# Moving the raw and the split weight rings of an encoder trunk to lower SBUF addresses, behind the activation buffers

## The chip, the core and the metric

The kernel runs on one core of one Trainium2 chip. The metric is the device time of one execution in microseconds; the text compares medians of several runs. One execution was also recorded by the hardware profiler, and everything said about single instructions comes from that recording.

## The reference

Two layers of a bidirectional hybrid encoder on a sequence of 256 positions with 2048 channels, all in float32, followed by a final RMSNorm. What matters for the time are the matrix products:

```python
hn = rms_norm(x, norm_w)
u = jnp.einsum("bsd,dn->bsn", hn, w_in) + b_in          # 2048 x 20496
q, k, v, o, z_a, gates, glu_a, glu_b, z_b, g_a, g_b = jnp.split(u, _OFFSETS, axis=-1)
...
y_a = jnp.einsum("bsw,wd->bsd", ya, w_a)                # 2048 x 2048, after a two-way mLSTM
y_b = jnp.einsum("bsw,wd->bsd", c, w_b)                 # 2048 x 2048, after a 31-tap convolution
merged = jax.nn.sigmoid(g_a) * y_a + jax.nn.sigmoid(g_b) * y_b
return x + jnp.einsum("bsd,de->bse", merged, w_out)     # 2048 x 2048
```

Between them stand four mLSTM heads of 512 channels in both directions, two depthwise convolutions, norms and gates.

## The kernel before, in words

**Split operands.** Every weight and every activation of the large products is split into a high part (rounded to the matmul's reduced 4-byte type, float32r) and a low part (what is left). A product is high x high + high x low + low x high. The activations lie in `Hs` (the normed input, later the merged branches) and `YC` (the branch outputs): 16 channel tiles of 512 columns each, 256 high ones and then 256 low ones.

**Pairs.** The unit of work is a pair of 128-column blocks of a weight matrix, 104 pairs in a layer and 208 in all. A pair's weights, 2048 rows by 256 columns, come in four quarters (`c` = 0 to 3) of 4 channel tiles each. SP loads a quarter into the raw ring `RAW` (L299, 512 KB). ACT casts it to the high part `WH` (L389), DVE subtracts that from the raw one for the low part `WL` (L690); both are halves of the split ring `W`. Each ring holds four quarters, one of each `c`, so quarter `c` of the next pair may be loaded and split as soon as TensorE has finished quarter `c` of this one. Semaphores carry this: `raw_in`, `hi_made`, `lo_made`, `multiplied`.

**The order long, long, short, short.** In `multiply` the weights are the stationary operand and the activations stream. For each channel tile TensorE runs two matmuls of 512 columns (high weights against both activation parts, one for each of the two blocks), then two of 256 columns (low weights against the high activations). Such a set of four is called a group below; a pair has 16 groups, and 192 of the 208 pairs run this way, 3072 groups.

```python
1250                    for kk in range(KQ):
...
1254                        for t in range(2):
1255                            mm(ps[:, 2 * q + t, :], WH[:, c, kk, t * P:t * P + P], act_in[:, kt, :],
1256                               start=(kt == 0), stop=False)
1257                        for t in range(2):
1258                            i = mm(ps[:, 2 * q + t, S:2 * S], WL[:, c, kk, t * P:t * P + P],
1259                                   act_in[:, kt, 0:S], start=False, stop=(kt == KT - 1))
```

**The turned order.** The other 16 pairs (two for each head, the values of the mLSTM) go through `multiply_turned`. There the activations are stationary and the weights stream, and a long matmul (L1274) alternates with a short one (L1276), 32 such twos in a pair, 512 in all. The 512 columns of the long one are two blocks of 256, one of `WH` and one of `WL`.

**The gate product.** Once in a layer the 16 gate columns of `w_in` are multiplied (L1334 and L1335): 16 times a long and a short matmul in turn, the stationary operand in `YC`, the streaming one in `Hs`. Neither touches the rings.

**Around them** stand small full-float32 matmuls in `px` (scores, L1393 and L1414; spreads and sums, L1320, L1384). ACT evicts and activates, DVE adds, convolves and norms.

**Addresses.** `sb` allocates the buffers one behind the other, in the order of the code (L122 to L146), and every buffer lies in all 128 partitions at the same byte offset. The order of the instructions on each engine doesn't depend on it.

Of the kernel before, what the change touches and what calls it, by code (L numbers as in the profile page):

```python
# [31 lines left out]
F32R = mybir.dt.float32r  # L32
# [4 lines left out]
P = 128  # L37
# [18 lines left out]
QC = 4  # L56
KQ = KT // QC
PC = 2 * P
# [53 lines left out]
def build_trunk(nc, x, norm_w, w_in, b_in, qk_conv_w, mlstm_norm_w, w_a, dw_w, dw_b,  # L112
                ln_w, ln_b, w_b, w_out, final_norm_w, out):
    with ExitStack() as ctx:
        def sb(name, shape, dt=F32):
            return ctx.enter_context(nc.sbuf_tensor(name, shape, dt))
# [5 lines left out]
        X = sb("X", [P, KT, S])  # L122
        Hs = sb("Hs", [P, KT, 2 * S], F32R)
        YC = sb("YC", [P, KT, 2 * S], F32R)
        CP = sb("CP", [P, KT * CW + PAD])
        M = sb("M", [P, KT, S])
        HEAD = sb("HEAD", [P, KT, S])
# [5 lines left out]
        ACC = sb("ACC", [P, 2, S])  # L133
        CWT = sb("CWT", [P, 2, DW_TAPS + 1])
        RR = sb("RR", [P, S])
        RAW = sb("RAW", [P, QC, KQ, PC])
        W = sb("W", [P, QC, 2, KQ, PC], F32R)
        PAR = sb("PAR", [P, L * PARS + KT])
        IDENT = sb("IDENT", [P, P])
        ONES = sb("ONES", [P, P])  # L140
# [6 lines left out]

        WH, WL = W[:, :, 0, :, :], W[:, :, 1, :, :]
        K_, V_, SO_ = (HEAD[:, HT * i:HT * (i + 1), :] for i in (0, 2, 3))
# [4 lines left out]

        GS = YC[:, 0:KT // 2, :].rearrange("p k (a g) -> p (k a) g", a=2)
        GLOW, GATES = HEAD[0:NG, 2 * HT + 1, :], HEAD[0:NG, 2 * HT + 2, :]
# [3 lines left out]
        SQUARES = HEAD[:, :, :].rearrange("p (s a) b -> p s (a b)", s=ST)  # L160
        PROWS = CP[:, 0:(L * PBLK + 1) * P].rearrange("p (b c) -> p b c", c=P)

# [95 lines left out]
        def conv_in(tile, tap):  # L258

            return CP[:, ds(tile * CW + tap, S)]  # L260

        def conv_out(tile, count):

            return CP[:, tile * CW:(tile + count) * CW].rearrange(
                "p (t c) -> p t c", c=CW)[:, :, PAD:CW]
# [5 lines left out]
        def buf(g):  # L271

            return (EW, QB)[g % 2]
# [9 lines left out]
        def _(sp):  # L283
# [10 lines left out]
            def load_pair(w, l, col, n):  # L294

                for c in range(QC):

                    sp.wait_ge(lo_made, n * QC + (c + 1))
                    sp.dma_start(RAW[:, c, :, :], w[l, :, c * KQ:(c + 1) * KQ, ds(col, PC)]  # L299
                                 ).then_inc(raw_in[c], 16)  # L300
# [40 lines left out]
        def _(pool):  # L341
# [5 lines left out]
                                    ).then_inc(ident_made, 1)  # L347
            nc.gpsimd.memset(YC[:, 0:KT // 2, :].bitcast(F32), 0.0).then_inc(gs_clear, 1)
            steps.mark(nc.gpsimd.memset(GC[:], 0.0))
            steps.mark(nc.gpsimd.memset(QPAD[:], 0.0))  # L350
            pool.wait_ge(rows_turned, 1)
            steps.mark(nc.gpsimd.memset(CP[:, 0:KT * CW].rearrange("p (t c) -> p t c", c=CW)
                                        [:, :, 0:PAD], 0.0))
            steps.mark(nc.gpsimd.memset(CP[:, KT * CW:], 0.0))
            steps.wait()
            pool.sem_inc(pads_made, 1)
            with pool.Fori(0, L) as l:

                n0 = pool.snap(l * NP)
                for c in range(QC):  # L360
                    pool.wait_ge(hi_made, n0 * QC + (c + 1))
                    nc.gpsimd.tensor_tensor(out=WL[:, c, :, :], in0=RAW[:, c, :, :],
                                            in1=WH[:, c, :, :].bitcast(F32), op=ALU.subtract
# [20 lines left out]
        def _(act):  # L384
            def split_hi(n, c):

                act.wait_ge(raw_in[c], n * 16 + 16)
                act.wait_ge(multiplied, n * QC + (c + 1))
                nc.scalar.copy(WH[:, c, :, :], RAW[:, c, :, :]).then_inc(hi_made, 1)  # L389

# [57 lines left out]
            with act.Fori(0, L) as l:  # L448
# [50 lines left out]
                with act.Fori(0, H) as h:  # L499
# [46 lines left out]
                    act.wait_ge(ya_made, u + 1)  # L546
                    nc.scalar.copy(YC[:, ds(h * HT, HT), 0:S], KV_).then_inc(ya_hi, 1)  # L547

# [36 lines left out]
                def cb_high(g):  # L585
                    act.wait_ge(cb_made, l * 4 + (g + 1))
                    nc.scalar.copy(YC[:, 4 * g:4 * g + 4, 0:S], buf(g)[:]).then_inc(cb_hi, 1)

# [94 lines left out]
        def _(dve):  # L683
# [3 lines left out]
            def split_lo(n, c):  # L687

                dve.wait_ge(hi_made, n * QC + (c + 1))
                v.tensor_tensor(WL[:, c, :, :], RAW[:, c, :, :], WH[:, c, :, :].bitcast(F32),  # L690
                                ALU.subtract).then_inc(lo_made, 1)
# [45 lines left out]
            with dve.Fori(0, L) as l:  # L737
# [59 lines left out]
                def glu_mul(tile, unit):  # L797

                    dve.wait_ge(glu_sig, unit)
                    dst = CP[:, ds(tile * CW, 2 * CW)].rearrange("p (t c) -> p t c", c=CW)  # L800
                    steps.mark(v.tensor_tensor(dst[:, :, PAD:CW], QB[:, 0:2, :], QB[:, 2:4, :],
# [79 lines left out]
                with dve.Fori(0, H) as h:  # L881
# [145 lines left out]
                    for t in range(HT):  # L1027
                        if t % 2 == 0:
# [6 lines left out]
                    dve.wait_ge(ya_hi, u + 1)  # L1035
                    v.tensor_tensor(YC[:, ds(h * HT, HT), S:2 * S], KV_,
                                    YC[:, ds(h * HT, HT), 0:S].bitcast(F32), ALU.subtract
                                    ).then_inc(ya_lo, 1)
# [198 lines left out]
        def _(pe):  # L1237
# [24 lines left out]
            def multiply_turned(n, k):  # L1262
# [3 lines left out]
                for c in range(QC):  # L1266
# [3 lines left out]
                    for kk in range(KQ):  # L1270
                        kt = c * KQ + kk
                        for s in range(ST):
                            bank = ps[:, 2 * q + s, :].rearrange("p (a b) -> p a b", a=2)
                            mm(bank, Hs[:, kt, s * P:(s + 1) * P], W[:, c, :, kk, :],  # L1274
                               start=(kt == 0), stop=False)
                            i = mm(bank[:, 1, :], Hs[:, kt, S + s * P:S + (s + 1) * P],  # L1276
                                   W[:, c, 0, kk, :], start=False, stop=(kt == KT - 1))
                    i.then_inc(multiplied, 1)
# [214 lines left out]
```

## Time and profile before

| what | before |
|---|---|
| median of 3 runs | 2509.46 us (2509.41 to 2509.69) |
| profiled execution, its own time | 2509.14 us |
| its span, first to last instruction | 2507.4 us |
| mean granted TensorE clock | 0.994 |
| busy: PE / PE weight loads / DVE / ACT | 99% / 86% / 77% / 52% |
| weights read from HBM | 441.59 MB in 2.5 ms |

The span is that of the instructions; the execution's time is 1.7 us longer. PE is TensorE streaming, PEld its weight loads, which lie beside the streaming. A matmul's recorded length contains its way through the array, which the next one overlaps, so the pace is read from starts, not from lengths.

### The profile page before, as it was taken

To read this page: it belongs to the slowest core of one execution; us is meant where nothing else is said; L and a number is where in the kernel's file an instruction comes from. 1 tells how busy PE (TensorE), PEld (TensorE's weight loads), DVE (VectorE), ACT (ScalarE), POOL (GpSimd) and SP (SyncE) were. 2 spreads that over 40 slices of the span, in tenths; PEclk is the share of its full clock that TensorE was granted. 3 is DMA by queue.
4 is the path that set the end of the run, shared out by engine and by line. 5 is a ranking of instruction groups with operands and counts; after the bars stand their busy time and mean duration, and the time that the engine had idled before them with its cause. 6 is when DMAs were issued, how large, how long until landed. Compare 5 with 4: busy or idle time off the path is not lost.

```text
span 2507.4 us, 43931 instructions
## 1 busy us (share of the span) xinstructions
PE 2474.0 (99%) x14063; PEld 2158.4 (86%) x14063; DVE 1937.5 (77%) x2872; ACT 1316.2 (52%) x1574; POOL 55.6 (2%) x43
## 2 busy tenths in 40 slices
PE   7999999999999999999989999999999999999998
PEld 6888888888888888888878888888888888888887
DVE  5788989898978786556568888888888877765565
ACT  4545454545465557555354454545454655665543
POOL 2000000000000000000010000000000000000000
PEclk9999999999999999999999999999999999999999
DMA  6566656565656666665546656555565666666654
GB/s 185 170 187 184 177 164 182 163 182 165 180 175 186 188 180 186 190 185 190 172 124 188 190 177 178 170 174 176 168 183 159 186 186 186 176 195 187 185 183 134
DMA packets 447922, 444.95 MB, mean 177 GB/s; under 512 B 17968, under 2 KB 445760, under 8 KB 447808
## 3 DMA queue, kind: packets, MB, share of 16 engines
q1 hardware_dynamic: 447808, 443.74, 59.3%
q8 instruction: 34, 0.56, 0.1%
q14 instruction: 80, 0.66, 0.1%
HBM read 441.59 MB, written 2.10 MB: 177 GB/s over the span
## 4 chain that ended last, share of the span: by engine, by line
PE 95%; issue 2%; DVE 2%; ACT 1%; SPq 0%; DVEq 0%; DMA 0%; ACTq 0%
PE ps L1255 55%; PE ps L1258 28%; PE ps L1274 5%; PE ps L1276 2%; PE px L1414 1%; PE px L1393 1%; PE px L1320 1%; DVE Hs L751 0%; DVE HEAD L1030 0%; PE px L1384 0%; SPq L289 0%; PE px L1334 0%; ACT YC L547 0%; ACT W L389 0%; PE px L1401 0%
## 5 line engine op out<-in xcount | busy, mean ns | idle before, releaser
L1255 PE MATMUL ps<-Hs,W 128*128 128x512 f32 x5120 | 1620.2, 398 | 9.0 <-DVE Hs L751 9.0
L690 DVE TENSOR_TENSOR W<-RAW,W 128x1024 fp32r<-128x1024 f32 x824 | 1019.3, 1243 | 439.8 <-ACT W L389 434.9
L389 ACT CAST W<-RAW 128x1024 fp32r<-128x1024 f32 x832 | 865.7, 1047 | 926.1 <-PE ps L1258 819.4
L1258 PEld LDWEIGHTS ps<-Hs,W 128*128 128x128 f32 x5120 | 964.1, 188 | 231.2
L1258 PE MATMUL ps<-Hs,W 128*128 128x256 f32 x5120 | 1024.6, 281 | 0.0
L1255 PEld LDWEIGHTS ps<-Hs,W 128*128 128x128 f32 x5120 | 790.7, 189 | 14.7 <-DVE Hs L751 10.8
L792 DVE SCALAR_TENSOR_TENSOR ACC<-CP,CWT,ACC 128x256 f32<-128x256 f32 x928 | 388.4, 478 | 0.0
L1255 PE MATMUL ps<-YC,W 128*128 128x512 f32 x1024 | 321.7, 395 | 0.0
L1258 PEld LDWEIGHTS ps<-YC,W 128*128 128x128 f32 x1024 | 192.3, 188 | 46.1
L1258 PE MATMUL ps<-YC,W 128*128 128x256 f32 x1024 | 204.6, 281 | 0.0
L1274 PE MATMUL ps<-W,Hs 128*128 128x512 f32 x512 | 179.9, 393 | 0.0
L1255 PEld LDWEIGHTS ps<-YC,W 128*128 128x128 f32 x1024 | 157.6, 188 | 0.0
L1276 PE MATMUL ps<-W,Hs 128*128 128x256 f32 x512 | 144.3, 282 | 0.0
L402 ACT ACTIVATE T<-ps,PAR 128x256 f32<-128x256 f32 x288 | 119.6, 465 | 0.0
L1274 PEld LDWEIGHTS ps<-W,Hs 128*128 128x128 f32 x512 | 96.1, 188 | 19.9
L1276 PEld LDWEIGHTS ps<-W,Hs 128*128 128x128 f32 x512 | 96.7, 189 | 0.2
L697 DVE TENSOR_TENSOR QB<-ps,T 128x512 f32<-128x512 f32 x112 | 76.5, 683 | 0.8 <-ACT T L398 0.8
L906 DVE SCALAR_TENSOR_TENSOR HEAD<-QPAD,PAR,HEAD 128x256 f32<-128x256 f32 x128 | 58.3, 524 | 0.2
L446 ACT ACT_TABLE_LOAD x42 | 53.9, 1283 | 0.8
L906 DVE SCALAR_TENSOR_TENSOR QB<-QPAD,PAR,QB 128x256 f32<-128x256 f32 x128 | 52.8, 480 | 1.4 <-DVE QB L906 1.4
L389 ACT ACT_TABLE_LOAD x38 | 48.8, 1283 | 0.7
L446 ACT ACTIVATE QB<-QB 128x512 f32<-128x512 f32 x48 | 30.3, 632 | 18.7 <-DVE QB L697 18.3
(179 smaller groups left out, 978.4 us busy)
## 6 DMA issues: line engine op xcount, KB each, us to landing
RAW<-in_w_in_dram SPq DMA_DIRECT2D x640, 512.0 KB, 3.7
RAW<-in_w_a_dram SPq DMA_DIRECT2D x64, 512.0 KB, 3.4
RAW<-in_w_b_dram SPq DMA_DIRECT2D x64, 512.0 KB, 3.4
RAW<-in_w_out_dram SPq DMA_DIRECT2D x64, 512.0 KB, 4.0
M<-in_x_dram SPq DMA_DIRECT2D x2, 1024.0 KB, 8.4
HEAD<-in_b_in_dram SPq DMA_DIRECT2D x8, 256.0 KB, 3.6
out_dram<-M SPq DMA_DIRECT2D x4, 512.0 KB, 2.9
CP<-in_dw_w_dram SPq DMA_DIRECT2D x3, 128.0 KB, 4.2
```

What stands on the lines that cost most here:

```text
L389: nc.scalar.copy(WH[:, c, :, :], RAW[:, c, :, :]).then_inc(hi_made, 1)
L402: i = nc.scalar.activation(T[:, q, t, :], ps[:, 2 * q + t, S:2 * S], ACT.Identity, bias=bias(t))
L446: nc.scalar.activation(where, where, ACT.Sigmoid).then_inc(done, 1)
L690: v.tensor_tensor(WL[:, c, :, :], RAW[:, c, :, :], WH[:, c, :, :].bitcast(F32), ALU.subtract).then_inc(lo_made, 1)
L697: v.tensor_tensor(dst, ps[:, 2 * q:2 * q + 2, 0:S], T[:, q, :, :], ALU.add).then_inc(pairs_out, 1)
L792: steps.mark(v.scalar_tensor_tensor(out=dst, in0=src, scalar=w, in1=ACC[:, t, :], op0=ALU.mult, op1=ALU.add))
L906: ins = v.scalar_tensor_tensor(out=dst[:, t, :], in0=src, scalar=w, in1=dst[:, t, :], op0=ALU.mult, op1=ALU.add)
L1255: mm(ps[:, 2 * q + t, :], WH[:, c, kk, t * P:t * P + P], act_in[:, kt, :], start=(kt == 0), stop=False)
L1258: i = mm(ps[:, 2 * q + t, S:2 * S], WL[:, c, kk, t * P:t * P + P], act_in[:, kt, 0:S], start=False, stop=(kt == KT - 1))
L1274: mm(bank, Hs[:, kt, s * P:(s + 1) * P], W[:, c, :, kk, :], start=(kt == 0), stop=False)
L1276: i = mm(bank[:, 1, :], Hs[:, kt, S + s * P:S + (s + 1) * P], W[:, c, 0, kk, :], start=False, stop=(kt == KT - 1))
L1320: i = mm(px[:, bank, at + s * P:at + (s + 1) * P], columns[:, s:s + 1].to_broadcast([P, P]), IDENT[:], start=True, stop=True)
```

## The change

Two lines move up. Nothing else differs: every engine has the same instructions in the same order.

```diff
         Hs = sb("Hs", [P, KT, 2 * S], F32R)
         YC = sb("YC", [P, KT, 2 * S], F32R)
+        RAW = sb("RAW", [P, QC, KQ, PC])
+        W = sb("W", [P, QC, 2, KQ, PC], F32R)
         CP = sb("CP", [P, KT * CW + PAD])
...
         RR = sb("RR", [P, S])
-        RAW = sb("RAW", [P, QC, KQ, PC])
-        W = sb("W", [P, QC, 2, KQ, PC], F32R)
         PAR = sb("PAR", [P, L * PARS + KT])
```

The byte offsets within a partition, as the two programs are built:

| buffer | bytes | before, starts at | changed, starts at | start modulo 1024, before / changed |
|---|---|---|---|---|
| X | 16,384 | 16,512 | 16,512 | 128 / 128 |
| Hs | 32,768 | 32,896 | 32,896 | 128 / 128 |
| YC | 32,768 | 65,664 | 65,664 | 128 / 128 |
| RAW | 16,384 | 168,352 | 98,432 | 416 / 128 |
| W | 32,768 | 184,736 | 114,816 | 416 / 128 |
| CP to RR (ten buffers) | 69,920 | 98,432 | 147,584 | all moved by 49,152, unchanged modulo 1024 |
| PAR and the rest | 8,708 | 217,504 | 217,504 | unchanged |

## Rows read from the trace of the kernel before

**Rows 1.** The page: span, busy time of each engine, busy tenths in 40 slices

```profile
span 2507.4 us, 43931 instructions
PE 2474.0 (99%) x14063; PEld 2158.4 (86%) x14063; DVE 1937.5 (77%) x2872; ACT 1316.2 (52%) x1574; POOL 55.6 (2%) x43
PE   7999999999999999999989999999999999999998
```

**Rows 2.** The page: the chain that ended last, by engine, by line

```profile
PE 95%; issue 2%; DVE 2%; ACT 1%; SPq 0%; DVEq 0%; DMA 0%; ACTq 0%
PE ps L1255 55%; PE ps L1258 28%; PE ps L1274 5%; PE ps L1276 2%; PE px L1414 1%; PE px L1393 1%; PE px L1320 1%; DVE Hs L751 0%; DVE HEAD L1030 0%; PE px L1384 0%; SPq L289 0%; PE px L1334 0%; ACT YC L547 0%; ACT W L389 0%; PE px L1401 0%
```

**Rows 3.** Busy time by window: an uninterrupted stretch in either layer

```profile
core 0: us, PE busy (x) PEld busy (x) DVE busy (x) ACT busy (x) POOL busy (x), PEclk, DMA share, GB/s
928.08:1252.70 324.62, 324.62 (x1850) 283.07 (x1849) 194.86 (x190) 180.58 (x214) 0.00 (x0) 1.00 0.61 186
2167.93:2492.54 324.61, 324.61 (x1850) 283.05 (x1849) 194.85 (x190) 180.57 (x214) 0.00 (x0) 1.00 0.58 179
```

**Rows 4.** Timeline of PE (start, length, line): first and last groups of the latter

```profile
2167.92 0.63 PE L1255 MATMUL ps<-Hs,W 128*128 128x512 f32 x2
...
2492.55 0.63 PE L1255 MATMUL ps<-Hs,W 128*128 128x512 f32 x2
```

**Rows 5.** What PE waited for, whole span, longest first (us, times, longest)

```profile
PE ps L1255 <- DVE Hs L751: 9.0, 6, 3.4
PE ps L1289 <- DMA M<-in_x_dram: 8.1, 1, 8.1
```

**Rows 6.** Timeline of PE: one turned pair, first, second and last long matmul

```profile
265.35 0.39 PE L1274 MATMUL ps<-W,Hs 128*128 128x512 f32 x1
265.58 0.28 PE L1276 MATMUL ps<-W,Hs 128*128 128x256 f32 x1
...
276.10 0.39 PE L1274 MATMUL ps<-W,Hs 128*128 128x512 f32 x1
```

**Rows 7.** Timeline of PE: the gate product, second to last long matmul

```profile
38.80 0.40 PE L1334 MATMUL px<-Hs,YC 128*128 128x512 f32 x1
39.03 0.28 PE L1335 MATMUL px<-Hs,YC 128*128 128x256 f32 x1
...
43.75 0.40 PE L1334 MATMUL px<-Hs,YC 128*128 128x512 f32 x1
```

**Rows 8.** Groups of PE by line in 2167.93 to 2492.54

```profile
L1255 PE MATMUL ps<-Hs,W 128*128 128x512 f32 x668 | 209.8, 395 | 0.0
L1258 PE MATMUL ps<-Hs,W 128*128 128x256 f32 x670 | 133.9, 281 | 0.0
L1255 PE MATMUL ps<-YC,W 128*128 128x512 f32 x256 | 80.4, 395 | 0.0
```

**Rows 9.** Timeline of PEld: one load to each matmul

```profile
270.78 0.19 PEld L1274 LDWEIGHTS ps<-W,Hs 128*128 128x128 f32 x1
270.90 0.19 PEld L1276 LDWEIGHTS ps<-W,Hs 128*128 128x128 f32 x1
271.13 0.19 PEld L1274 LDWEIGHTS ps<-W,Hs 128*128 128x128 f32 x1
```

**Rows 10.** The splits of ACT and DVE, whole span, and who waits

```profile
L690 DVE TENSOR_TENSOR W<-RAW,W 128x1024 fp32r<-128x1024 f32 x824 | 1019.3, 1243 | 439.8 <-ACT W L389 434.9
L389 ACT CAST W<-RAW 128x1024 fp32r<-128x1024 f32 x832 | 865.7, 1047 | 926.1 <-PE ps L1258 819.4 <-PE ps L1276 97.5 <-DMA RAW<-in_w_in_dram 5.2
L1036 DVE TENSOR_TENSOR YC<-HEAD,YC 128x1024 f32 x8 | 9.8, 1225 | 1.9 <-ACT YC L547 1.9
ACT W L389 <- DMA RAW<-in_w_in_dram: 5.2, 6, 1.0
```

## The prediction

> **What bounds the kernel now.** First the page: PE is busy 99% of the span and in every slice but the first and a few others full [rows 1]. The chain that ended last is PE for 95%, and 83% of it are the two lines of the long, long, short, short order, 7% the two turned ones [rows 2]. So I asked next whether PE waits there or is simply streaming. In two stretches of 324.6 us, one in each layer, PE has no idle time at all, at a granted clock of 1.00 (the 2.4 GHz level) [rows 3]. The longest waits of PE in the whole span are 9.0 and 8.1 us in total [rows 5]. Nothing feeds PE too late. What is left is the pace of the stream itself, and that has to be read from starts, since lengths overlap.
>
> The second stretch runs from 2167.92 to 2492.55 us [rows 4]. By the code it holds 15 groups of one pair, 64 of the four z_B pairs and 384 of the 24 pairs of g_B, w_B and w_out, 463 starts and so 462 intervals: 324.63 / 462 = 702.7 ns for a group of 2 x 512 + 2 x 256 = 1536 columns. At one column for each beat of 2.4 GHz it would be 640 ns. The stream thus loses 62.7 ns in a group, 9%, or 15.7 ns for each matmul. It is this loss, 3072 x 62.7 ns = 193 us of the kernel, that placement could touch.
>
> **The change part by part.** It removes no instruction and adds none; it moves none on any engine, SP's and POOL's queues included. It changes addresses only. Who touches the moved bytes:
>
> *DMA into RAW, ACT's cast, DVE's subtraction.* The cast takes 1047 ns on average and the subtraction 1243 ns; a subtraction of the same size between buffers that start at 128 modulo 1024 takes 1225 ns [rows 10]. If the rings' new start had any effect here, 18 ns x 824 = 15 us of DVE would go. It counts as nothing, because the work is covered: within the two stretches DVE is busy 195 and ACT 181 of 325 us [rows 3], and the cast waited 917 us for PE to release the ring, against 5.2 us for the load [rows 10]. What would uncover it: in a group time of 0.70 us a quarter takes PE 2.8 us, the load share is 0.61 [rows 3], and the cast and the subtraction one after the other take 2.3 us but run three quarters ahead. They would have to be slowed by far more than the 18 ns in question. The bound above and below is 0 us.
>
> *The ten buffers CP to RR* move by 49,152 bytes and keep their start modulo 1024. They are read and written by the small work, of which only the float32 matmuls in px lie on the chain, about 1% a line [rows 2]. I take 0; they run a fixed sequence, and no row shows one of them depending on an address.
>
> *PE's own reads of W.* This is the only term with a price. Is there a row which shows that the pace depends on where operands lie? Three streams can be compared, all of 4-byte float32r, all with one weight load beside each matmul [rows 9]:
> - the group order, W stationary (start 416 modulo 1024), Hs streaming (128): 702.7 ns, so 351.3 ns for a long and a short [rows 4];
> - the turned order, Hs stationary (128), W streaming (416): 31 intervals from 265.35 to 276.10, 346.8 ns [rows 6];
> - the gate product, YC stationary (128), Hs streaming (128): 14 intervals from 38.80 to 43.75, 353.6 ns [rows 7].
>
> The last two have the same order (long, short), the same column counts and the same clock, and differ by 6.8 ns, 2%. They differ in the operands: roles, the split of the long stream into two blocks, and placement. So the pace is not fixed by shape alone. What does not matter is also visible. In the gate product the distance between the two operands changes with every step by 1024 bytes, and in a pair it runs through four values of kk and, between Hs and YC, through a further 32,768 bytes; yet the mean length with YC is 395 ns as with Hs [rows 8]. Large steps of distance are therefore without effect. What the change does alter is the small part: W goes from 416 to 128 modulo 1024, the phase that YC and Hs have. It makes every pair of operands lie like those of the gate product, which is the slowest of the three.
>
> I bound the term by these rows. Upper row: the group order takes the pace of the gate product, 2 x 353.6 = 707.2 ns, +4.5 ns x 3072 = +13.8 us, and the turned one too, +6.8 ns x 512 = +3.5 us; sum +17.3 us. Lower row: the group order takes the turned pace, 693.6 ns, -9.1 x 3072 = -28.0 us, the turned one stays. Above the upper row: if the phase costs the group order the same factor that separates the two alternating streams, 353.6 / 346.8 = 1.020, it is 716.5 ns, +42.4 us, with the turned term +46 us. Below the lower one: all of the loss goes, -193 us, and 512 x (346.8 - 320) = -14 us.
>
> I take the upper row, +17.3 us, because it is the one stream in the trace that lies as all of them will. The sum is made against the profiled execution: 2509.1 + 17.3 = 2526.4 us; that execution stands 0.3 us under the median of the runs, which changes nothing. Everything lies on the path, since PE never waits where the groups run.
>
> A rule speaks against this. The Trainium skill, in the page TensorE: Matmul & The Clock Gate, section Part 2: What happens when you issue a matmul, says that the weight load and the streaming operand have independent read ports, so that loading the next weights takes no read bandwidth from the running matmul. By it placement is worth nothing and the sum is 0. The same page's section Back-to-back issue gap gives N / 2.4 + 2.5 ns, 650 ns for a group, and the trace does not agree with that for this type: 702.7 ns. No run here shows yet what makes the difference.
>
> **The rivals.**
>
> *The pace doesn't depend on the placement* (the change has no effect): 2509 us. For it: the pace is steady over all kk, both activation buffers and both layers [rows 3, 8], and the 6.8 ns can come from the two-block stream or from the roles alone. Against it: there is a loss of 9% that the column count doesn't explain, and an operand-dependent difference of 2%. The rule on read ports above is this rival's.
>
> *The phase was the costly thing before, and falls away*: the reads of W started 32 bytes off a 64-byte boundary, now they start on one as all other buffers do. If such a start costs a part of each weight load or stream, the group order goes down to the turned pace: 2481 us. For it: the group order alone has W stationary, and it loses more than the turned one. Against it: the gate product has no odd start and is slower still [rows 7]. It decides if a group falls under 702 ns.
>
> *The whole loss is a collision* between the two reads of PE that new addresses avoid: 2509 - 207 = 2302 us. Against it: the gate product has other distances and loses as much.
>
> *The phase costs the group order the full factor*: 2555 us. This is the forecast's mechanism at its upper price.
>
> *A feeder becomes the bound*, because DMA, ACT and DVE now work in the bytes next to those that PE streams: it would show as waits of PE for `lo_made`. Against it: the slack above, and the two stretches have the same pace whatever DVE and ACT do. Under 1%, and it is in no case below.
>
> **How the numbers follow.** A change of 0.2%, 5 us, is about what a measurement of this kernel can tell from none. The forecast, 2526 us, has 0.37; the same mechanism at the full factor 0.08. No dependence has 0.27, the odd start falling away 0.24, the whole loss going 0.04. So slower by over 0.2% is 0.45, within 0.2% 0.27, faster 0.28. The range reaches from a little under the turned pace, 2478 us, to the full factor, 2556 us; left out are the case of 2302 us and what lies beyond either end, together under 0.2. As cases of both signs hold much of the chance: the forecast's own range is 2515 to 2540 us.
>
> **What would show it right or wrong.** In the changed profile the instruction counts and the granted clock should be the same, and PE should still have no idle time in the long stretches. Right: a group of 705 to 710 ns, and a turned two of 353 ns instead of 347; the gate product unchanged at 353.6 ns, since neither of its operands moved. If the group moves but the turned two doesn't, it is the stationary read that feels the address; if only the turned one moves, the streaming read. A group at 702.7 ns means no dependence, one near 693 ns the odd start. The forecast fails as a whole if the time changes while the pace of the groups doesn't: then a wait has come up that I excluded. The casts and subtractions may come out some ns shorter or longer, without any effect on the end.

## The result, and the profile after

The changed kernel is faster: a median of 2492.49 us (2491.69 to 2493.51, four runs) against 2509.43 us (2507.43 to 2509.69, four runs) of the kernel before beside it, a ratio of 0.9932 with a 95% interval of 0.992 to 0.9945. That is 17 us less; the forecast was 17 us more.

The page first: the span, busy times and busy slices of PE of the changed kernel.

```profile
span 2490.0 us, 43931 instructions
PE 2455.4 (99%) x14063; PEld 2141.2 (86%) x14063; DVE 1934.5 (78%) x2872; ACT 1317.2 (53%) x1574; POOL 55.6 (2%) x43
PE   7999999999999999999989999999999999999998
```

The same instructions, the same shares as in [rows 1], 17.4 us less span, and 18.6 us less busy time of PE. Now the two long stretches by window (busy time and count of each engine, clock, DMA share, GB/s), which answer to [rows 3]:

```profile
921.36:1243.21 321.85, 321.85 (x1850) 280.81 (x1849) 194.55 (x190) 180.86 (x214) 0.00 (x0) 1.00 0.61 187
2153.45:2475.30 321.85, 321.85 (x1850) 280.81 (x1849) 194.57 (x190) 180.84 (x214) 0.00 (x0) 1.00 0.59 180
```

PE is busy without a break again, at the same granted clock of 1.00, with the same counts; DVE and ACT do the same work in the same time. Only the stretch is 2.8 us shorter. The timeline of PE gives the pace, first and last group of the second stretch, as in [rows 4]:

```profile
2153.44 0.40 PE L1255 MATMUL ps<-Hs,W 128*128 128x512 f32 x1
...
2475.30 0.40 PE L1255 MATMUL ps<-Hs,W 128*128 128x512 f32 x1
```

321.86 / 462 = 696.7 ns for a group, where it was 702.7 ns. 3072 groups x 6.0 ns = 18.4 us: that is the whole result, and a little more.

A little more, because the turned pairs went the other way, in part. Two of them, first and last long matmul from the second one on (30 intervals between the rows):

```profile
262.02 0.39 PE L1274 MATMUL ps<-W,Hs 128*128 128x512 f32 x1
...
272.42 0.39 PE L1274 MATMUL ps<-W,Hs 128*128 128x512 f32 x1
```

```profile
385.01 0.40 PE L1274 MATMUL ps<-W,Hs 128*128 128x512 f32 x1
...
395.61 0.40 PE L1274 MATMUL ps<-W,Hs 128*128 128x512 f32 x1
```

10.40 / 30 = 346.7 ns and 10.60 / 30 = 353.3 ns. In the kernel before all 16 turned pairs ran at 346.7 to 347.1 ns. Here eight run at one of these paces and eight at the other, 512 x 3.0 ns = 1.5 us lost. 18.4 - 1.5 = 16.9 us is what was measured, to within half a microsecond.

And the gate product, whose operands the change doesn't touch, changed its pace (14 intervals):

```profile
38.56 0.39 PE L1334 MATMUL px<-Hs,YC 128*128 128x512 f32 x1
...
43.42 0.39 PE L1334 MATMUL px<-Hs,YC 128*128 128x512 f32 x1
```

4.86 / 14 = 347.1 ns against 353.6 ns in [rows 7]. (With two decimals over 14 intervals the quotient is good to 0.7 ns; the starts to the nanosecond give 346.6 ns.) This row should have stayed. It was the first sign that the row on which the forecast was built isn't what I took it for.

The splits stood still: subtraction 1243 ns and cast 1048 ns, against 1243 and 1047 in [rows 10].

```profile
L690 DVE TENSOR_TENSOR W<-RAW,W 128x1024 fp32r<-128x1024 f32 x824 | 1018.1, 1243 | 426.0 <-ACT W L389 420.4
L389 ACT CAST W<-RAW 128x1024 fp32r<-128x1024 f32 x832 | 866.5, 1048 | 905.3 <-PE ps L1258 795.1 <-PE ps L1276 99.1 <-DMA RAW<-in_w_in_dram 5.3
```

### The profile page after: what moved, and what is told of

The parts are those of the page before. It is cut to its first block, busy times and chain, and to the rows that moved or that the text cites. A ratio compares the mean times of both kernels' runs of the same rounds, so it can differ in the third digit from the quotient of the medians.

```text
span 2490.0 us, 43931 instructions
## 1 busy us (share of the span) xinstructions
PE 2455.4 (99%) x14063; PEld 2141.2 (86%) x14063; DVE 1934.5 (78%) x2872; ACT 1317.2 (53%) x1574; POOL 55.6 (2%) x43
## 4 chain that ended last, share of the span: by engine, by line
PE 95%; issue 2%; DVE 2%; ACT 1%; SPq 0%; DVEq 0%; DMA 0%; ACTq 0%
PE ps L1255 55%; PE ps L1258 27%; PE ps L1274 5%; PE ps L1276 2%; PE px L1414 1%; PE px L1393 1%; PE px L1320 1%; DVE Hs L751 0%; DVE HEAD L1030 0%; PE px L1384 0%; SPq L289 0%; PE px L1334 0%; ACT YC L547 0%; ACT W L389 0%; PE px L1401 0%
## 5 line engine op out<-in xcount | busy, mean ns | idle before, releaser
L1255 PE MATMUL ps<-Hs,W 128*128 128x512 f32 x5120 | 1617.7, 397 | 9.6 <-DVE Hs L751 9.6
L690 DVE TENSOR_TENSOR W<-RAW,W 128x1024 fp32r<-128x1024 f32 x824 | 1018.1, 1243 | 426.0 <-ACT W L389 420.4
L389 ACT CAST W<-RAW 128x1024 fp32r<-128x1024 f32 x832 | 866.5, 1048 | 905.3 <-PE ps L1258 795.1
L1258 PE MATMUL ps<-Hs,W 128*128 128x256 f32 x5120 | 1007.2, 278 | 0.0
L1255 PEld LDWEIGHTS ps<-Hs,W 128*128 128x128 f32 x5120 | 781.6, 189 | 15.2 <-DVE Hs L751 11.2
L1255 PE MATMUL ps<-YC,W 128*128 128x512 f32 x1024 | 321.6, 395 | 0.0
L1255 PEld LDWEIGHTS ps<-YC,W 128*128 128x128 f32 x1024 | 155.9, 189 | 0.0
```

## The experiments

"Distance" below is the start of W less the start of Hs, modulo 256; YC and Hs stand in the same phase. The kernel before has 32, the changed one 0.

### Chance, region, or the small part of the start

The two kernels once more, unchanged:

> The kernel before once more, unchanged, as its own profile beside the others. If the pace of the stream is a property of the program (theories 1 and 2), it shows again 702.7 ns for a group, 346.8 ns for a turned two and 353.6 ns for a two of the gate product, and 2509 us. If the pace is a state that an execution or a chip falls into by chance (theory 3), some of these numbers differ and the time can come near 2492 us.

> The changed kernel once more, unchanged. Theories 1 and 2: a group of 696.7 ns, a two of the gate product of 346.7 ns, 2492 us, ratio 0.993. Theory 3 (a state by chance): the paces can be those of the kernel before, 2509 us.

Then the change taken apart. The rings low, but in the old phase:

```diff
         YC = sb("YC", [P, KT, 2 * S], F32R)
+        sb("GAP0", [P, 72])
         RAW = sb("RAW", [P, QC, KQ, PC])
         W = sb("W", [P, QC, 2, KQ, PC], F32R)
+        sb("GAP1", [P, 184])
         CP = sb("CP", [P, KT * CW + PAD])
```

> The rings stay behind the activation buffers, but 288 bytes further on, so that RAW and W start at 416 modulo 1024 as in the kernel before; all other buffers keep their start modulo 1024. Theory 1 (the small part of the start counts, 416 against 128): the pace of the kernel before, a group of 702.7 ns and a two of the gate product of 353.6 ns, 2509 us, ratio 1.000. Theory 2 (the region counts, behind the activations against the top): the pace of the changed kernel, 696.7 ns, 2492 us, ratio 0.993. Theory 3 (chance): no rule.

The rings high, but in the new phase:

```diff
         RR = sb("RR", [P, S])
+        sb("GAP0", [P, 184])
         RAW = sb("RAW", [P, QC, KQ, PC])
         W = sb("W", [P, QC, 2, KQ, PC], F32R)
+        sb("GAP1", [P, 72])
         PAR = sb("PAR", [P, L * PARS + KT])
```

> The rings stay at the top as in the kernel before, but 736 bytes further on, so that RAW and W start at 128 modulo 1024 as in the changed kernel. Theory 1 (the small part of the start): the pace of the changed kernel, a group of 696.7 ns, 2492 us, ratio 0.993. Theory 2 (the region): 702.7 ns, 2509 us, ratio 1.000. Theory 3 (chance): no rule.

Measured beside the kernel before (2510.15 us): before again 2509.30 us, after again 2493.81 us, low in the old phase 2510.39 us (ratio 1.0001, 0.9989 to 1.0012), high in the new phase 2493.79 us (0.9936, 0.9914 to 0.9959). The timelines of PE over the same 462 groups, first of the rings low in the old phase, then high in the new one (in both the added lines make L1257 of L1255):

```profile
2168.59 0.40 PE L1257 MATMUL ps<-Hs,W 128*128 128x512 f32 x1
...
2493.22 0.39 PE L1257 MATMUL ps<-Hs,W 128*128 128x512 f32 x1
```

```profile
2154.32 0.40 PE L1257 MATMUL ps<-Hs,W 128*128 128x512 f32 x1
...
2476.17 0.40 PE L1257 MATMUL ps<-Hs,W 128*128 128x512 f32 x1
```

324.63 / 462 = 702.7 ns and 321.85 / 462 = 696.6 ns, the 696.7 ns of the changed kernel to within the rounding of the rows. The move of some 70,000 bytes is worth nothing; the part of the start below 1024 is worth all of it. The group pace isn't chance either: two profiles of each kernel gave the same 702.7 and 696.7 ns. But the gate product was. In the second profile of the changed kernel it reads

```profile
38.89 0.40 PE L1334 MATMUL px<-Hs,YC 128*128 128x512 f32 x1
...
43.84 0.40 PE L1334 MATMUL px<-Hs,YC 128*128 128x512 f32 x1
```

4.95 / 14 = 353.6 ns, the pace of the kernel before, with the addresses of the run that showed 347.1.

### Which bytes, and whose

Four kernels from the changed one. A gap of 32 bytes ahead of the rings, then one of 448 (in these and in all later ones a second gap, behind W or, with RAW alone, ahead of it, makes up 1024 bytes with the first and so keeps the other buffers' phase):

```diff
-        RAW = sb("RAW", [P, QC, KQ, PC])
-        W = sb("W", [P, QC, 2, KQ, PC], F32R)
+        sb("GAP0", [P, 8]); RAW = sb("RAW", [P, QC, KQ, PC])
+        W = sb("W", [P, QC, 2, KQ, PC], F32R); sb("GAP2", [P, 248])
```

> The changed kernel with a gap of 32 bytes ahead of RAW: RAW and W start at 160 modulo 1024, on an odd multiple of 32 bytes, the activations at 128. Theory 1a (what counts is the 32-byte bit, whether the start is a multiple of 64): slow as before, a group of 702.7 ns, 2510 us. Theory 1b (a larger part of the distance counts, such as the 256 in the 288 between 416 and 128): a group of 696.7 ns or another number, 2493 us.

> The changed kernel with a gap of 448 bytes (64 + 128 + 256) ahead of RAW: the starts stay multiples of 64 but RAW and W stand at 576 modulo 1024, the activations at 128. Theory 1a (only the 32-byte bit counts): fast, a group of 696.7 ns, 2493 us. Theory 1b (the larger bits count): not 696.7 ns; 702.7 ns and 2510 us if any difference from the activations' phase is what costs.

The gap of 32 bytes ahead of Hs instead, so that all operands shift together:

```diff
-        Hs = sb("Hs", [P, KT, 2 * S], F32R)
+        sb("GAP3", [P, 8]); Hs = sb("Hs", [P, KT, 2 * S], F32R)
```

> The changed kernel with a gap of 32 bytes ahead of Hs: Hs, YC, RAW and W all start at 160 modulo 1024, on an odd multiple of 32 bytes, and have the same phase to each other. Theory A (the relation of the two operands that TensorE reads counts): fast, a group of 696.7 ns, 2493 us. Theory B (each operand's own start counts, a start off a multiple of 64 costs): slow, a group of 702.7 ns or more, 2510 us or above since now the streaming operands are odd too, and the gate product, which had never an odd operand, gets a pace it has not shown yet.

And RAW alone in the old phase:

```diff
-        RAW = sb("RAW", [P, QC, KQ, PC])
-        W = sb("W", [P, QC, 2, KQ, PC], F32R)
+        sb("GAP0", [P, 72]); RAW = sb("RAW", [P, QC, KQ, PC])
+        sb("GAP1", [P, 184]); W = sb("W", [P, QC, 2, KQ, PC], F32R)
```

> The changed kernel with RAW alone at 416 modulo 1024 and W at 128. TensorE never reads RAW. If the effect is in TensorE's reads of W (my theory), it is fast, a group of 696.7 ns, 2493 us. If it comes from the DMA's writes of RAW or from the cast and the subtraction that read it, it is slow, 702.7 ns and 2510 us.

Beside the kernel before at 2509.79 us: 32 bytes 2509.12 us, 448 bytes 2478.92 us (ratio 0.9874, 0.9845 to 0.9903), all shifted 2492.97 us (0.9938), RAW alone 2491.64 us (0.9934). The timelines, of the one with 448 bytes and of the one with all shifted:

```profile
2141.24 0.40 PE L1255 MATMUL ps<-Hs,W 128*128 128x512 f32 x1
...
2460.04 0.39 PE L1255 MATMUL ps<-Hs,W 128*128 128x512 f32 x1
```

```profile
2154.87 0.40 PE L1255 MATMUL ps<-Hs,W 128*128 128x512 f32 x1
...
2476.73 0.40 PE L1255 MATMUL ps<-Hs,W 128*128 128x512 f32 x1
```

318.80 / 462 = 690.0 ns, and 321.86 / 462 = 696.7 ns. Two readings follow. The kernel with every operand on an odd multiple of 32 bytes is as fast as the one with none: what counts is the distance between TensorE's two operands, not the start of either (theory A; tried at one distance, 0, and with one shift, 32 bytes). And RAW, which TensorE never reads, has no part in it, so it isn't the loads, nor the reads of RAW by the splits. But the theory that only the 32-byte bit counts fell with 448 bytes: some 14 us better than the changed kernel, which no theory of mine gave.

The splits also write W, and those writes moved along with it in every kernel. The traces answer that part. In the second stretch there are groups during which neither a cast nor a subtraction is writing W: 46 of the 462 in the kernel before, with a mean of 703.3 ns, and 47 in the changed one, with 696.8 ns, against 702.7 and 696.7 ns for all (single groups scatter by 5 ns in the kernel before, so a mean of 46 is good to 0.8 ns). During 55 and 48 groups no DMA packet is under way; their means are 703.1 and 696.6 ns. In the whole run there are 53 and 52 groups with neither, with 703.2 and 697.0 ns. The two paces differ just as much when no other engine writes W and no load is under way.

### The order of the groups

The same edit in two kernels, in the kernel before (distance 32) and in the changed one (distance 0). Every short matmul now follows the long one of its block:

```diff
                         for t in range(2):
                             mm(ps[:, 2 * q + t, :], WH[:, c, kk, t * P:t * P + P], act_in[:, kt, :],
                                start=(kt == 0), stop=False)
-                        for t in range(2):
+
                             i = mm(ps[:, 2 * q + t, S:2 * S], WL[:, c, kk, t * P:t * P + P],
                                    act_in[:, kt, 0:S], start=False, stop=(kt == KT - 1))
```

> The kernel before (W at 416 modulo 1024) with the order long, short, long, short in the groups. The turned pairs have this order and the same odd relation and ran at a steady 346.7 to 347.1 ns for a long and a short in every profile so far. If the order and the relation set the pace, a group takes 693.4 to 694.1 ns, 3072 x 9 ns = 27 us less than before: 2482 us, faster than the changed kernel. If the turned pace comes from the roles or from its stream in two blocks, the group stays at 702.7 ns or higher, 2510 us.

> The changed kernel (W at 128 modulo 1024, as the activations) with the order long, short, long, short in the groups. The turned pairs with this relation showed two paces, 346.7 or 353.3 ns from pair to pair, and the gate product too. If order and relation set the pace, the groups fall into either, from pair to pair, 693.3 or 706.7 ns, so on average between 2481 and 2523 us, and runs of the same kernel spread more than others; near 2500 us. If the order doesn't matter: 696.7 ns and 2493 us.

Beside the kernel before at 2507.52 us the first came out at 2514.63 us (ratio 1.003, 1.0018 to 1.0042): my expectation of 2482 us was wrong. The second came at 2504.54 us with eight runs from 2493.28 to 2515.29 us, a spread of 22 us where no other kernel spreads by more than 6 in its own set of runs. That was expected. Its profiled run, one of 2494.59 us, suggests why; the timeline of PE in two stretches, 90 intervals of a long and a short each:

```profile
716.82 0.39 PE L1255 MATMUL ps<-Hs,W 128*128 128x512 f32 x1
...
748.02 0.39 PE L1255 MATMUL ps<-YC,W 128*128 128x512 f32 x1
```

```profile
1319.79 0.40 PE L1255 MATMUL ps<-Hs,W 128*128 128x512 f32 x1
...
1351.59 0.40 PE L1255 MATMUL ps<-Hs,W 128*128 128x512 f32 x1
```

31.20 / 90 = 346.7 ns and 31.80 / 90 = 353.3 ns, for the same instructions at the same addresses. At these two distances the alternating groups have two paces and fall into one or the other. With distance 0 about two thirds of that run were at the fast one; with distance 32 (the first kernel) about a tenth, the mean 352.6 ns. That the share changes from run to run is inferred from the spread, as one run of each kernel was recorded. The order long, long, short, short is steadier. At five of the eight distances below (0, 32, 64, 128, 192) its 192 pairs, waits left out, lie about one pace, none more than 4 ns off. At the other three a second pace stands out: at 160 bytes 49 pairs ran at 700.0 ns and 140 at 706.7, at 96 bytes 13 at 706.7 instead of 703.3, and at 224 bytes 8 at 706.7 instead of 693.4.

### The rest of the 256 bytes

> The changed kernel with a gap of 64 bytes ahead of RAW: W stands 64 bytes off the activations' phase modulo 512 (gap 448 stood 64 short of it and gave 690.0 ns). Theory P1 (any distance that is a multiple of 64 but not 0 modulo 512 is the fast one): 690 ns, 2479 us. Theory P2 (a scale of its own for each distance, no rule by bits): another number, between 690 and 703 ns.

> The same with 128 bytes. Theory P1: 690 ns, 2479 us. Theory P3 (only the 64-byte bit counts beside the 32-byte one, so that 128 is like 0): 696.7 ns, 2493 us.

> The same with 256 bytes. Theory P1: 690 ns, 2479 us. Theory P3: like 0, 696.7 ns, 2493 us. The kernel before stood at 288, gap 32 at 32, both at 702.7 ns, so the 256-byte bit made no difference there; if it makes none here either, P3 is favoured.

> The same with 480 bytes, 32 short of the activations' phase. All odd multiples of 32 so far (32, 288) gave 702.7 ns. If the 32-byte bit alone makes a start slow: 702.7 ns, 2509 us. If the 64-byte bit shifts this pace too, as it may have at 448: another number, about 696 ns and 2494 us.

> The changed kernel with a gap of 192 bytes ahead of RAW. So far the distances 0 and 256 gave the same pace (696.7 ns), and 32 and 288 too (702.7 ns). If the pace has a period of 256 bytes, 192 is the same place as 448: a group of 690.0 ns, 2479 us, ratio to the kernel before 0.988, and turned twos of a steady 353.0 ns. If the 256-byte bit matters here, another number.

> The same with 160 bytes. No theory of mine gives its value; the distances 128, 192 and 224 around it gave 696.7, 690.0 and 693.4 ns. If the pace goes smoothly between neighbours: 690 to 697 ns, 2479 to 2494 us. If an odd multiple of 32 costs as at 32: 700 ns or above, 2502 us.

> The same with 96 bytes. Neighbours 64 and 128 gave 693.3 and 696.7 ns. Smooth: 693 to 697 ns, 2486 to 2494 us. Odd multiples of 32 slow below 128: about 702.7 ns, 2509 us.

All the kernels with the order long, long, short, short in one table. The group's pace is worked out as above from the 462 groups of the second stretch, the turned one from the starts within a pair. In a turned pair W is the streaming operand, so the distance counted from the streaming to the stationary one has the other sign there:

| distance modulo 256 | kernels | group, ns | a turned two, ns | median, us |
|---|---|---|---|---|
| 0 | changed (twice), high in the new phase, all shifted, RAW alone, gap 256 | 696.7 | 346.7 or 353.3 | 2491.6 to 2493.8 |
| 32 | before (twice), low in the old phase (288), gap 32 | 702.7 | 346.7 to 347.1 | 2509.1 to 2510.4 |
| 64 | gap 64 | 693.3 | 353.3 | 2486.6 |
| 96 | gap 96 | 703.3 | 350.2 | 2512.7 |
| 128 | gap 128 | 696.7 | 350.8 | 2495.3 |
| 160 | gap 160 | 706.7 (mean over all groups, waits left out: 704.9) | 346.7 | 2518.0 |
| 192 | gap 448, gap 192 | 690.0 | 353.0 | 2478.9, 2476.1 |
| 224 | gap 480 | 693.4 | 352.8 or 353.4 | 2486.8 |

The period of 256 bytes rests on three places measured at two distances each: 0 and 256, 32 and 288, 192 and 448 agree. P1 (every multiple of 64 but 0 is fast) fell with 128; P3 (only the 64-byte bit) fell with 128 against 0 and 64 against 192. "Every odd multiple of 32 is slow" fell with 224, and a smooth course between neighbours fell with 96 and 160. There is no simple rule in the column, and I have none. One regularity stands in the numbers: in beats of 2.4 GHz 690.0, 693.3, 696.7, 700.0, 703.3 and 706.7 ns are 1656, 1664, 1672, 1680, 1688 and 1696, whole multiples of eight. Only the 702.7 ns of distance 32 falls between them.

The gap of 192 bytes beats both kernels: 2476.07 us (2474.0 to 2478.91) beside 2509.85 us, ratio 0.9865 (0.9849 to 0.9882), 33.8 us less. Its timeline and its busy time by window:

```profile
2141.77 0.40 PE L1255 MATMUL ps<-Hs,W 128*128 128x512 f32 x1
...
2460.57 0.39 PE L1255 MATMUL ps<-Hs,W 128*128 128x512 f32 x1
```

```profile
2141.78:2460.57 318.79, 318.79 (x1850) 280.53 (x1849) 194.42 (x190) 180.33 (x214) 0.00 (x0) 1.00 0.60 182
```

318.80 / 462 = 690.0 ns, 12.6 ns under the kernel before: 3072 x 12.6 = 38.7 us, less 512 x 6 ns = 3.1 us for the turned pairs, 35.6 us, where 33.8 us was measured. PE still has no idle time, so the feeders keep up with this pace as well.

## Why the prediction was wrong, point by point

**What bounds the kernel** was right: the pace of PE's own stream, on the path one for one, with nothing that feeds it too late. The result is the pace of the groups times 3072 and the turned pace times 512, to half a microsecond. In the other kernels with the order long, long, short, short the same sum meets the median to 5 us; the largest misses are 4.7 us with the gap of 448 bytes (35.6 us by the sum, 30.9 us measured, two runs) and some 4 us with 160, where the second stretch has only the slower of its two paces.

**The loads, the casts and the subtractions at 0 us**, right. The 18 ns by which the ring's subtraction is longer than its neighbour did not come from the start either: 1243 ns in both. (The buffers from CP to RR, called ten, are eleven.)

**Large steps of distance are without effect**, right: the region is worth nothing, and 256 bytes more or less neither.

**The term that failed is the price of PE's reads of W, in sign.** I took +4.5 ns for a group because the gate product "is the one stream in the trace that lies as all of them will", at 353.6 ns for a long and a short. Measured is -6.0 ns: the term stands in the sum as +13.8 us and came out as -18.4 us. Two things were wrong with that step. The gate product has the order long, short, and such a stream has two paces, 346.7 and 353.3 ns, at the very same addresses; the trace held 32 of its twos, all in the slow one, and I read a chance state as a property of the placement. The unchanged gate product at 347.1 ns in the changed kernel and 353.6 ns in its second profile shows that. Over all 19 profiles its 38 passes (one a layer) had 353.6 ns 24 times, 346.6 or 346.7 ns 11 times and something between three times, though Hs and YC never changed their distance. And a pace of one order doesn't carry over to the other. The second kernel with alternating groups has the gate product's order and distance: it took 693.3 or 706.7 ns for a group, and the order long, long, short, short at that same distance takes 696.7 ns, neither of them. At the distance of 192 the groups have their fastest pace, and the turned pairs one of their slowest.

**The argument that the pace must depend on placement**, 346.8 against 353.6 ns, was therefore no evidence, though what it was to prove is true. I had the same two streams in two layers only; the steady 346.7 to 347.1 ns of sixteen turned pairs made the comparison look firmer than it was.

**The turned term** (+3.5 us) had the right sign; it was 1.5 us, as half of the pairs stayed at the fast pace. How many stay there is chance: in the second profile of the changed kernel six pairs were fast and ten slow. The sign that was to tell the stationary read from the streaming one (only the groups move, or only the turned twos) gave no answer, as both moved.

**The rivals.** "The odd start falls away" had the sign and was 11 us too low in the time, but not for its reason: with Hs, YC, RAW and W all 32 bytes off a multiple of 64 the kernel is as fast. Nor were RAW and W the only buffers with such a start: the length of QPAD, 2080 bytes, puts T, ROWS, ACC, CWT and RR behind it on one as well, in both kernels. "No dependence" is refuted by fifteen kernels that differ in nothing but the places of their buffers. On the rule of independent read ports (the Trainium skill, the page TensorE: Matmul & The Clock Gate, section Part 2: What happens when you issue a matmul) the trace gives this much: by it placement should be worth nothing, and the group pace goes from 690.0 to 706.7 ns with the distance alone. The section's sentence is about the weight load and the running matmul, and no run here had a stream without weight loads, so that the two reads collide is argued and not shown. What is shown is that their distance counts, and, where it was tried, not the start of the one or the other. The prediction's 650 ns for a group are an estimate by a formula of the Trainium skill, the page TensorE: Matmul & The Clock Gate, section Back-to-back issue gap, which the section gives for a matmul alone, without the weight load that stands beside every matmul here.

What stays open: the mechanism, the values at the eight distances, why an alternating order (and the other one at some distances) has two paces, and the remaining 50 ns over 640 in a group.

## What to carry to other kernels

Where TensorE is busy without a break and still over its column count, try the distance between the stationary and the streaming buffers, in steps of 32 bytes over 256: the best place was worth 1.35% here over the kernel before and the worst cost 0.3%, so an allocation added for another reason can move the time by as much unseen. Read the pace from starts over hundreds of matmuls; and before a stream in the trace serves as a model for another one, look at it in a second profile.

## What the runs showed of the hardware that I had not expected

- With the order long, long, short, short the pace of float32r matmuls (2 x 512 + 2 x 256 columns, one weight load each) depends on the distance between the two operands' starts: 690.0 ns at 192 bytes to 706.7 ns at 160 (where a quarter of the pairs ran at 700.0), with a period of 256 as far as measured.
- Alternating long and short matmuls at distance 0 have two paces, 346.7 and 353.3 ns, for the same instructions (the turned pairs at 96 and 128 bytes had one in between, 350.2 and 350.8 ns); a stream keeps one for tens of microseconds, and the kernel built all in that order spread over 22 us from run to run.
- The pace is unmoved by DVE, ACT and the DMA, which write and read in the bytes next to the operands: groups without a write to W by either engine and groups without a DMA packet have the mean of all, within the scatter (703.3 and 703.1 against 702.7 ns before, 696.8 and 696.6 against 696.7 ns changed).
